# Splitting each weight unit into its two parts in two halves, in a two-layer trunk on one core

## The reference, cut to what matters

```python
for l in range(2):
    mod = silu(c) @ w_mod[l] + b_mod[l]            # 6 x 1024 columns: shift, scale, gate, twice
    h = rms_norm(x, g) * (1 + scale) + shift
    proj = h @ w_in[l]                             # 1024 x 5120
    o_a = stick_breaking_attention(...) @ w_proj_sb
    o_b = moba_attention(...) @ w_proj_moba
    y = (sigmoid(g_a) * o_a + sigmoid(g_b) * o_b) @ w_out
    x = x + gate * rms_norm(y, g_post)
    h = rms_norm(x, g) * (1 + scale) + shift
    y = swiglu(h) if l == 0 else moe_top2_of_8(h)  # inner width 3584, each of 8 experts too
    x = x + gate * rms_norm(y, g_post)
```

## Time and profile before

| | |
|---|---|
| median of the runs | 1797.66 us |
| profiled execution | 1799.94 us, its span 1798.2 us |
| mean granted TensorE clock | 0.977 |
| TensorE busy | 1669.9 us (93%), 8014 products |
| VectorE busy | 1388.5 us (77%), of it L290 993.5 us in 436 instructions |
| ScalarE busy | 1109.2 us (62%), of it L285 833.3 us in 436 instructions |
| GpSimd busy | 64.9 us (4%) |
| HBM read | 510.30 MB, 284 GB/s over the span |

### The profile page before, as it was taken

How to read it: one execution, slowest core, us unless ns; L and a number is a source line. 1 busy time by engine, 2 the same in 40 slices (tenths; PEclk the granted TensorE clock), 3 DMA queues, 4 the chain that set the end, 5 groups by cost and what they waited for, 6 DMA issues and landing times.

```text
span 1798.2 us, 23115 instructions
## 1 busy us (share of the span) xinstructions
PE 1669.9 (93%) x8014; PEld 1373.0 (76%) x8014; DVE 1388.5 (77%) x1258; ACT 1109.2 (62%) x966; POOL 64.9 (4%) x194
## 2 busy tenths in 40 slices
PE   4989979999979999699999999999999999999996
PEld 4967757777769777578878788788788788788785
DVE  5946867777776456668888978888888888788888
ACT  3555443333335554367777777777777777778775
POOL 0010010000000100410000000000000000000000
PEclk9999989999989999699999999999999999999998
DMA  8954646667648334069989989889899799899894
GB/s 332 374 196 167 234 164 259 248 265 280 247 154 325 118 110 171 24 242 370 368 312 375 353 315 365 334 345 364 306 375 378 294 364 374 305 366 367 316 373 163
DMA packets 72878, 512.05 MB, mean 285 GB/s; under 512 B 9011, under 2 KB 10236, under 8 KB 10876
## 3 DMA queue, kind: packets, MB, share of 16 engines
q1 hardware_dynamic: 71184, 510.18, 74.8%
q10 hardware_dynamic: 1644, 1.22, 0.2%
HBM read 510.30 MB, written 1.06 MB: 284 GB/s over the span
## 4 chain that ended last, share of the span: by engine, by line
PE 81%; DVE 8%; ACT 5%; issue 3%; POOL 2%; DMA 1%; ACTq 0%; DVEq 0%; POOLq 0%
PE ps L1215 25%; PE ps L1217 24%; PE ps L1216 24%; DVE wlo L290 4%; ACT whi L285 3%; PE ps L1438 2%; PE ps L1547 1%; DVE raw L299 1%; DMA qk<-in_rel_bias 1%; PE ps L1305 1%; PE ps L1236 1%; DVE x L773 1%; ACT vals L621 1%; ACT L285 0%; PE ps L1571 0%
## 5 line engine op out<-in xcount | busy, mean ns | idle before, releaser
L290 DVE TENSOR_TENSOR wlo<-raw,whi 128x2048 fp32r<-128x2048 f32 x436 | 993.5, 2290 | 251.1 <-ACT whi L285 249.2
L285 ACT ACTIVATE whi<-raw 128x2048 fp32r<-128x2048 f32 x436 | 833.3, 1915 | 294.4 <-PE ps L1217 294.2
L1215 PE MATMUL ps<-whi,hhi 128*128 128x512 f32 x1376 | 549.6, 399 | 13.2 <-DVE wlo L290 4.8
L1216 PE MATMUL ps<-whi,hlo 128*128 128x512 f32 x1376 | 540.2, 393 | 0.0
L1217 PE MATMUL ps<-wlo,hhi 128*128 128x512 f32 x1376 | 539.4, 392 | 0.0
L1215 PEld LDWEIGHTS ps<-whi,hhi 128*128 128x128 f32 x1376 | 261.0, 190 | 80.0 <-DVE wlo L290 13.7
L1217 PEld LDWEIGHTS ps<-wlo,hhi 128*128 128x128 f32 x1376 | 260.6, 189 | 56.0
L1216 PEld LDWEIGHTS ps<-whi,hlo 128*128 128x128 f32 x1376 | 261.0, 190 | 52.6 <-issue 1.0
L1215 PE MATMUL ps<-whi,ohi 128*128 128x512 f32 x624 | 249.6, 400 | 2.6 <-DVE wide L894 1.7
L1217 PE MATMUL ps<-wlo,ohi 128*128 128x512 f32 x624 | 243.8, 391 | 0.0
L1216 PE MATMUL ps<-whi,olo 128*128 128x512 f32 x624 | 243.1, 390 | 0.0
(11 more groups left out here) (209 smaller groups left out, 1091.6 us busy)
## 6 DMA issues: line engine op xcount, KB each, us to landing
raw<-in_w_moe SPq DMA_DIRECT2D x336, 1024.0 KB, 6.5
raw<-in_w_pre_moe SPq DMA_DIRECT2D x100, 1024.0 KB, 4.9
raw<-in_w_mod_units SPq DMA_DIRECT2D x48, 1024.0 KB, 5.3
x<-in_x ACTq DMA_DIRECT2D x1, 1024.0 KB, 9.5
bias<-dist_scratch SPq DMA_DIRECT2D x1, 1024.0 KB, 8.3
out<-x SPq DMA_DIRECT2D x2, 512.0 KB, 2.7
condb<-in_c SPq DMA_DIRECT2D x1, 512.0 KB, 5.4
qk<-in_bucket_onehot ACTq DMA_DIRECT2D x1, 49.4 KB
```

Source lines behind the costliest of these rows:

```text
L285: nc.scalar.activation(whi[:, s % SPLIT, :], raw[:, slot(s), :], ACT.Copy).then_inc(hi_done, 1)
L290: nc.vector.tensor_tensor(wlo[:, s % SPLIT, :], raw[:, slot(s), :], whi[:, s % SPLIT, :].bitcast(F32), ALU.subtract).then_inc(lo_done, 1)
L1215: nc.tensor.matmul(out, a_hi, b_hi, start=first, stop=False, **kw)
L1216: nc.tensor.matmul(out, a_lo, b_hi, start=False, stop=False, **kw)
```

## The change

The high and the low part are each made by two instructions of 1024 columns instead of one of 2048. `hi_done` and `lo_done` now count halves, so that every value waited for is doubled. TensorE waits for the first half ahead of its first product with a unit (`use`), and for the second ahead of the first product that reads it (`rest`).

```diff
             wait_at_least(act, unit_used, number(s, r) - SPLIT + 1)
-            nc.scalar.activation(whi[:, s % SPLIT, :], raw[:, slot(s), :], ACT.Copy).then_inc(hi_done, 1)
+            for h in range(2):
+                part = slice(h * D, (h + 1) * D)
+                nc.scalar.activation(whi[:, s % SPLIT, part], raw[:, slot(s), part], ACT.Copy).then_inc(hi_done, 1)
 
         def split_lo(dve, s, r=0):
-            dve.wait_ge(hi_done, number(s, r) + 1)
             wait_at_least(dve, unit_used, number(s, r) - SPLIT + 1)
-            nc.vector.tensor_tensor(wlo[:, s % SPLIT, :], raw[:, slot(s), :], whi[:, s % SPLIT, :].bitcast(F32),
-                                    ALU.subtract).then_inc(lo_done, 1)
+            for h in range(2):
+                part = slice(h * D, (h + 1) * D)
+                dve.wait_ge(hi_done, number(s, r) * 2 + (h + 1))
+                nc.vector.tensor_tensor(wlo[:, s % SPLIT, part], raw[:, slot(s), part],
+                                        whi[:, s % SPLIT, part].bitcast(F32), ALU.subtract).then_inc(lo_done, 1)
...
-                sp.wait_ge(lo_done, number(s, r) - RAW + 1)
+                sp.wait_ge(lo_done, number(s, r) * 2 - (2 * RAW - 2))
...
-                        sp.wait_ge(lo_done, m + 1)
+                        sp.wait_ge(lo_done, 2 * m + 2)
...
-                pe.wait_ge(lo_done, number(s, r) + 1)
+                pe.wait_ge(lo_done, number(s, r) * 2 + 1)
+
+            def rest(s, r=0):
+                pe.wait_ge(lo_done, number(s, r) * 2 + 2)
...
                     for k in range(4):
+                        if c == 0 and k == 2:
+                            rest(s, r)
                         ins = three(bank[banks + c][:], hhi[:, 4 * kh + k, cs], hlo[:, 4 * kh + k, cs], w_hi[:, k, :],
...
                 w_hi, w_lo = unit(s, D)
                 for k in range(2):
+                    if k:
+                        rest(s, r)
```

More of the change, by code:

```diff
@@ L1255, in rows_step @@
                         for k in range(4):
+                            if c == 0 and k == 2:
+                                rest(s)
                             ins = three(bank[banks[c]][:], a_hi[:, kcs + k, cs], a_lo[:, kcs + k, cs], w_hi[:, k, :],
@@ L1266, in first_blocks @@
                         if j == 2:
+                            rest(base + k)
                             for c in range(C):
@@ L1374, in mixer @@
                                 for k in range(4):
+                                    if cc == 0 and k == 2:
+                                        rest(s)
                                     kk = 4 * kh + k
@@ L1452, in dense_down @@
                             for k in range(2):
+                                if k and half == 0:
+                                    rest(s + part, r)
                                 hk = hidden_half(b).start + 2 * part + k
```

## The result

The changed kernel takes 1776.86 us (median of 4 runs, 1775.53 to 1777.88), the one before 1798.03 beside it: a ratio of 0.988, 95% interval 0.9863 to 0.9898. That is 21 us won where 16 were forecast; the time lies inside the range, close to its lower end. The profiled execution took 1776.28 us with a span of 1774.5.

A forecast was written before the change was run, and what follows sets the result against it. TensorE's own work was taken to set the pace, so only its gaps could be won: 8.9 + 3.0 + 0.8 + 1.6 + 0.7 + 0.6 + 0.4 = 16.0 us, giving a median of 1781.7 us, range 1776 to 1790.

The forecast's parts named there:

- first units: Program start: unit 0's low part 1.9 us earlier, halves costing VectorE 0.08 for each unit; 1.6 us won.
- masking step: Attention: the split ahead of GpSimd's four masks ends 0.7 us earlier, and so do the masks; 0.7 us won.
- end of both mixers: Short gaps behind splits at the mixers' ends, not counted singly: 0 to 1.5 us, of which 0.4 taken.
- dense blocks: Second transposition behind L881: VectorE free 0.6 us earlier in five blocks; 3.0 us won.
- expert starts: Two low-part gaps at each of seven starts, 1.2 us together, plus 0.5 for the first expert: 8.9 us won.
- tail: After the last expert: its last split lets VectorE reach the low part of the sum 0.6 us earlier; 0.6 won.
- the sum as it stands: Main case, all terms holding: 13 to 19 us won, chance 0.60.
- The whole low part 0.7 earlier by overlap: Each split: with VectorE idle before it, whole `wlo` ends after 3.5 us, 0.7 earlier, because the two engines overlap.
- the rival that the second half comes last: Second half late at every gap, TensorE stops six products later; only the overlap's 0.7 stays: 1785 us, no separate chance.
- dear halves: Rival: VectorE pays 0.15 to 0.25 us for each split; gain of 12, 1785.7 us; chance 0.15.
- The next wait takes over: Rival at expert starts: waits for L1018, then L876 stay put, returning the first gap; gain 10.5, 1787.2 us; chance 0.12.
- TensorE pays nothing for the wait: 436 added mid-unit waits cost nothing, products stay 0.23 us apart; the rival of a price had chance 0.08.

The follow-up runs named there:

- second pair: Repeat runs with second profiles, both kernels unaltered: the changed kernel 1777.69 us (0.9881), the one before 1798.99 us (1.0003).
- the first experiment: Changed kernel, but TensorE waits for both halves of the low part ahead of its first product with a unit: 1780.71 us, 0.9897 of the kernel before.
- quarters: Changed kernel with four parts of 512 columns on both engines, TensorE waiting for two and for four: 1785.15 us, 0.9925 of the kernel before.
- mid-unit wait alone: Kernel before plus a second, always satisfied wait of TensorE in the middle of each of 436 units: 1799.04 us, ratio 0.9995.

## Why the prediction was right, step by step

The second pair of profiles, taken apart by the starts of the same products:

| stage | forecast, us | second pair, us |
|---|---|---|
| first units | 1.6 | 1.4 |
| masking step | 0.7 | 0.3 |
| end of both mixers | 0.4 | 1.4 (0.7 each) |
| dense blocks | 3.0 | 3.0 |
| end of the dense layer | 0.8 | 0.7 |
| expert starts | 8.9 | 10.2 |
| tail | 0.6 | 2.6 |
| not placed: stretches at the low clock and where they fall | 0 | 1.5 |
| sum | 16.0 | 21.1 |

- *The size*: 21 lies above the 13 to 19 that I had called the sum as it stands, and close to the end of the range. Of the 5.1 us too few in the sum, 2.0 are the tail, 1.3 the expert starts, 1.0 the mixers, and 1.5 are not placed; the first units and the masking step came out 0.6 smaller together. That the time still lies in the range is in part luck: the tail's surplus is explained only in part (below).
- *Gaps behind the low part*: right. 15 waits gone, 10.2 us with what stands behind them: 1.3 for each of seven starts (1.2 forecast) and 1.1 for the first (0.5). There was a third gap in each start that the waits don't list, since the modelled end of the product before hides it: at 1145.12 us a unit's first two products of the kernel before come 0.33 and 0.34 us after the ones ahead of them, in the changed kernel (1130.10) 0.23 and 0.22, which is 0.2 us of the 1.3.
- *The whole low part 0.7 earlier by overlap*: right, and it is the mechanism. My sum named TensorE's first half and its 1.9 us as the cover of the expert gaps; that cover is there but was not needed. The overlap alone covers them, as the first experiment shows; I had written that only under the rival that the second half comes last.
- *Queued half: 0.08 on VectorE for each unit*: right, 0.07 in the queue and 26 / 436 = 0.06 over the whole program. The "dear halves" rival is out, and quarters were no dearer for each instruction.
- *The next wait takes over*: it did not in the change. At the start shown L880 is 15.58 us ahead of L876 of the kernel before, while TensorE ahead of that start leads by 14.92: VectorE came 0.66 us earlier, 0.55 to 0.6 forecast. The wait grew from 1.08 to 1.15 us only. It did take over as soon as VectorE's earlier start was taken away.
- *Dense blocks*: right, 0.7 for four of them. One, at 411 us, won 0.1, since a copy of the gate stands in front of its split.
- *TensorE pays nothing for the wait*: right.
- *Masking step*: sized 0.7, was 0.3 (TensorE's wait fell from 3.12 to 2.80 us). The split ahead did end earlier, but the masks are held by the two mod columns behind it: two of the four take 1.22 and 1.27 us in the changed kernel and 1.27 each in the one before, where only the first one's 0.55 against 0.29 was the split's.
- *The tail* was the term mis-sized most. TensorE's wait for L1055 fell from 2.84 to 2.20 us as forecast. But 1.25 us in which it waited for nothing that the profile shows are gone too, the sums behind moved up, and the last products ran at the full clock instead of the lower level (0.33 us apart instead of 0.43 in the second pair). Part of this looks like chance: that empty time is 1.52 us in the first profile of the kernel before and 0.70 in the one with the mid-unit wait alone, and the changed kernel with the whole unit waited for has 0.67. How much follows from the change stays open.

## What to carry to other kernels

When two engines work on a tile one after the other, halves on both can pay when an instruction of the second waits for one of the first on the path; halves on one of them paid next to nothing here. Look at what is next in the second engine's queue, since that decides whether the gap closes or moves; and try the order of that queue first: moving one product ahead of one split won half as much as the change, with no instruction added. Two parts were enough here, four lost again.

## What the runs showed of the hardware

GpSimd and VectorE shut each other out more than I had counted. A mask of GpSimd takes 0.29 us otherwise. In the changed kernel one stands for as long as a half of the low part; timeline of both:

```profile
96.27 1.30 DVE L294 TENSOR_TENSOR wlo<-raw,whi 128x1024 fp32r<-128x1024 f32 x1
```

```profile
96.45 1.27 POOL L1091 TENSOR_SCALAR_AFFINE_SELECT at<-at 128x128 f32<-128x128 f32 x1
```

The half itself took 1.30 instead of 1.22 us. In the kernel before one stands for a whole low part:

```profile
85.77 2.29 DVE L290 TENSOR_TENSOR wlo<-raw,whi 128x2048 fp32r<-128x2048 f32 x1
```

```profile
85.85 2.36 POOL L1087 TENSOR_SCALAR_AFFINE_SELECT at<-at 128x128 f32<-128x128 f32 x1
```

The Trainium skill says so in "SBUF — State Buffer", section "SBUF: two separate sides": an instruction of VectorE with two inputs in SBUF and one of GpSimd that reads SBUF exclude each other for its whole length, and this trace agrees. Halves did not let GpSimd in sooner for more than one mask here: behind the first half it got one in, and that one was held by the second. Of 67 masks 6 took over 0.4 us before and 13 in the changed kernel; all together they took 25.0 and 31.7 us (27.5 with quarters). How much of this is the length of VectorE's instructions, and how much where they fall, isn't shown.

The instruction L696 that took 2.73 or 4.39 us on the second 128 tokens took 0.75 on the first, 1.5 us before. Beside it GpSimd clears tiles, one MEMSET after the other (1.8 us, four of 0.5 and one of 0.3). In all 13 profiles it is the same: where L696 took 2.73 us (four of them) the third MEMSET took 1.06 instead of 0.52, and where it took 4.38 (nine) none was longer. So it looks as if VectorE came in between two MEMSETs in the former and only behind the last in the latter; both kinds of kernel, before and changed, had either.

The other part of what differs between two profiles of the same code is, in these traces, the clock: after the same wait of 2.8 us TensorE had no stretch at the lower level of 1.2 GHz in one profile of the changed kernel and one of 6.8 us in the other (granted clock 0.50 from 106 to 112 us, where the first had 1.00), 3 us of difference. The first product behind the wait, in both:

```profile
105.71 0.71 PE L1301 MATMUL ps<-qk 64*128 64x256 f32 x4 [2.80 <-POOL at L1091]
```

```profile
105.79 1.23 PE L1301 MATMUL ps<-qk 64*128 64x256 f32 x4 [2.81 <-POOL at L1091]
```
